# The last gated MLP's gate and value products as seven half-size block products

## The reference, cut to what matters

```python
def swiglu_ffn(h, w_ffn_in, w_ffn_out):
    gate, up = jnp.split(h @ w_ffn_in, 2, axis=-1)
    return (jax.nn.silu(gate) * up) @ w_ffn_out
...
    x = _layer_norm(DEEPNORM_ALPHA * x + (1.0 + g_m) * y, ln1_g[l], ln1_b[l])
    h = _normalize(x) * (1.0 + sc_f) + sh_f
    y = swiglu_ffn(h, w_ffn_in[l], w_ffn_out[l])
    x = _layer_norm(DEEPNORM_ALPHA * x + (1.0 + g_f) * y, ln2_g[l], ln2_b[l])
```

## Time and profile before

| | us |
|---|---|
| median of 3 runs (lowest, highest) | 3415.74 (3415.02, 3417.43) |
| span of the profiled execution | 3414.4 |
| PE busy in it | 3335.1 |
| POOL, DVE, ACT busy in it | 1914.8, 1622.3, 757.2 |
| the last MLP from the end of its opening to the last norm | 3044.3 to 3396.2 |

### The profile page before, as it was taken

One profiled execution on the slowest core, in us unless ns is written; L12 is line 12 of the kernel. 1 busy time (PEld: TensorE's weight loads), 2 busy tenths in 40 slices (PEclk: granted clock), 3 DMA queues, 4 the chain that ended last, 5 costly groups with the idle time before them and its releaser, 6 DMA issues.

```text
span 3414.4 us, 46593 instructions
## 1 busy us (share of the span) xinstructions
PE 3335.1 (98%) x19518; PEld 2647.3 (78%) x19518; DVE 1622.3 (48%) x2658; ACT 757.2 (22%) x1595; POOL 1914.8 (56%) x1555
## 2 busy tenths in 40 slices
PE   8999999999999999999999998999999999999998
PEld 6767788986778888888788787788887776778886
DVE  6544434548444344343532756463346756541123
ACT  2242011347420112000202532110003225120001
POOL 7526666731266666766665003776675645756662
PEclk9999999999999999999999999999999999999999
DMA  5203333230033343332233002333324634422221
GB/s 169 87 25 111 108 127 136 79 103 26 26 111 108 126 136 98 125 123 92 93 96 108 8 3 81 124 99 99 96 90 163 203 99 174 142 75 99 87 99 37
DMA packets 253681, 340.76 MB, mean 100 GB/s; under 512 B 9761, under 2 KB 186145, under 8 KB 250913
## 3 DMA queue, kind: packets, MB, share of 16 engines
q1 hardware_dynamic: 230960, 301.51, 27.2%
q10 hardware_dynamic: 22512, 36.28, 3.1%
HBM read 308.15 MB, written 25.43 MB: 98 GB/s over the span
## 4 chain that ended last, share of the span: by engine, by line
PE 88%; DVE 6%; POOL 2%; ACT 2%; DMA 1%; issue 1%; ACTq 0%; DVEq 0%; SPq 0%; POOLq 0%
PE bank L125 86%; PE bank L128 2%; POOL wlo L148 1%; DVE scr L148 1%; DMA sq<-gates 1%; DVE st L163 0%; POOL whi L155 0%; DVE p L155 0%; POOL raw L148 0%; ACT L143 0%; DVE al L148 0%; DMA raw<-in_w_mlp_in 0%; ACT ah L143 0%; DVE x L148 0%; DVE BK L148 0%
## 5 line engine op out<-in xcount | busy, mean ns | idle before, releaser
L148 POOL TENSOR_TENSOR wlo<-raw,whi 128x512 fp32r<-128x512 f32 x962 | 1297.4, 1379 | 20.1
L155 POOL TENSOR_SCALAR whi<-raw 128x1024 fp32r<-128x1024 f32 x481 | 548.6, 1159 | 1354.7 <-PE bank L125 668.5
L125 PE MATMUL bank<-ah,whi 128*128 128x512 f32 x2408 | 958.8, 398 | 11.3 <-ACT ah L143 4.5
L125 PE MATMUL bank<-ah,wlo 128*128 128x512 f32 x2408 | 951.8, 395 | 0.0
L125 PE MATMUL bank<-al,whi 128*128 128x512 f32 x2408 | 940.4, 395 | 1.0 <-DVE al L158 1.0
L125 PEld LDWEIGHTS bank<-ah,whi 128*128 128x128 f32 x2408 | 451.7, 188 | 132.3 <-ACT ah L143 8.2
L125 PEld LDWEIGHTS bank<-al,whi 128*128 128x128 f32 x2408 | 451.5, 188 | 112.3 <-DVE al L158 1.8
L125 PEld LDWEIGHTS bank<-ah,wlo 128*128 128x128 f32 x2408 | 451.7, 188 | 110.3 <-issue 0.2
L125 PE MATMUL bank<-hh,whi 128*128 128x512 f32 x1040 | 412.5, 397 | 0.0
L125 PE MATMUL bank<-hl,whi 128*128 128x512 f32 x1040 | 410.9, 395 | 0.0
L125 PE MATMUL bank<-hh,wlo 128*128 128x512 f32 x1040 | 410.8, 395 | 0.0
(11 more groups left out here) (456 smaller groups left out, 3978.1 us busy)
## 6 DMA issues: line engine op xcount, KB each, us to landing
raw<-in_w_in SPq DMA_DIRECT2D x34, 1024.0 KB, 5.3
raw<-in_w_mlp_in SPq DMA_DIRECT2D x32, 1024.0 KB, 5.5
raw<-in_w_mlp_out SPq DMA_DIRECT2D x32, 1024.0 KB, 7.3
raw<-in_w_ada SPq DMA_DIRECT2D x24, 1024.0 KB, 5.3
raw<-in_ffn_w_gate SPq DMA_DIRECT2D x22, 1024.0 KB, 5.5
raw<-in_ffn_w_up SPq DMA_DIRECT2D x22, 1024.0 KB, 5.4
raw<-in_ffn_w_down SPq DMA_DIRECT2D x22, 1024.0 KB, 5.0
raw<-in_w_ffn_in SPq DMA_DIRECT2D x22, 1024.0 KB, 5.1
```

Of the source, the lines that this page charges most:

```text
L125: return self.eng.matmul(out, lhsT, rhs, start=start, stop=stop, skip_group_check=True)
L148: return IDLE if self.eng is None else self.eng.tensor_tensor(out, a, b, op)
L155: return self.eng.tensor_scalar(out, a, s1, s2, op0, op1)
```

## The change

Groups 1 to 5 of the last MLP no longer take their gate and value slabs through `lin`. These 18 slabs (four in each of groups 1 to 4, two in group 5) are loaded as before, but as the kind "pairs". A slab of 1024 x 256 weights is seen as 2 x 2 blocks A11, A12 (output tile 0, input rows 0-511 and 512-1023), A21, A22 (output tile 1), and the activations as 2 x 2 blocks of 512 features x 256 tokens. The 2 x 2 block product is done with seven block products (Strassen's form in Winograd's order) instead of eight. Each of the seven is 4 x 3 = 12 matmuls of 128x128 weights on 256 columns, so a slab has 84 of them. Details:

- POOL makes four block sums S1 = A22+A21, S2 = S1-A11, S3 = A11-A21, S4 = A12-S2 (each 128x512; S1, S2, S4 into a tile each, one copy of each for all slabs; S3 in place of A21) and the low parts of A11 and A12. It does S1, the two low parts, S2, S3, S4, in that order.
- ACT makes the seven high parts (each 128x512) in the order A11, A12, S1, S2, A22, S4, S3, and DVE the other five low parts.
- The `whi` and `wlo` buffers are cut into 12 pieces of 128x512; a slab uses seven, and a piece is free when the product that read its predecessor is done.
- PE puts the seven products (0 to 6) into three banks as halves of 256 columns. Product 3 adds onto product 0, 5 onto 2 and 6 onto 3; ACT copies the intermediate states to SBUF (128x256 each: "P1" after product 0, "P5" after product 2, "U2" after 3, "P4" after 4), and PE waits for P1 before product 3, for P5 before product 5 and for U2 before product 6. DVE finishes the two tiles with an addition each (`pair_first_dve` after product 5, `pair_second_dve` after product 6).
- Silu now works on the finished tile in SBUF, and the product of gate and value is SBUF by SBUF into `scr`.
- Once, in group 0, the activations' combinations are made: ACT writes eight value tiles in `ln1_act`, DVE four sums of 128x1024, ACT four high parts, DVE four low parts (products 2, 3, 4 and 6 use them). Those of product 2 overwrite a quarter of `ah` and `al` and so wait for the last matmul of group 0's value slab.

The order in which ACT and DVE interleave this work is written out in `paired_act` and `paired_dve`. The rest of the program issues the same instructions as before. The diff, cut to its core:

```diff
+    BLOCKS = "A11", "A12", "S1", "S2", "A22", "S4", "S3"
+    OPENS, CLOSES = (0, 1, 2, 4), (1, 4, 5, 6)
...
+    def pair_pe(self, e, key, W, c0, after=None, first=False):
+        P, C, D = self.P, self.C, self.D
+        src = W[0:1024, c0:c0 + 256].rearrange("(k p) n -> p k n", p=128)
+        i, _ = self.load("pairs", src, 8, 256, after)
...
+        banks = []
+        for n in range(3):
+            bank, free = self.ps.take(key, n)
+            e.wait_ge(*free)
+            banks.append(bank)
+        a, c, b, m = banks[0][:, 0:256], banks[0][:, 256:512], banks[1][:, 0:256], banks[2][:, 0:256]
+        for n, out in enumerate((b, a, c, b, m, c, b)):
+            e.wait_ge(*self.low_at(s, n))
+            if first and n in (2, 3, 4, 6):
+                e.wait_ge(*D.at(key[0], "tokens", n))
+            if n == 3:
+                e.wait_ge(*C.at(key, "P1"))
+            elif n == 5:
+                e.wait_ge(*C.at(key, "P5"))
+            elif n == 6:
+                e.wait_ge(*C.at(key, "U2"))
+            hi, lo = self.piece(self.whi, q + n), self.piece(self.wlo, q + n)
+            for k in range(4):
+                xh, xl = self.token_block(n, k)
+                e.mm(out, hi[:, k, :], xh, k == 0 and n in self.OPENS, False)
+                e.mm(out, hi[:, k, :], xl, False, False)
+                t = e.mm(out, lo[:, k, :], xh, False, k == 3 and n in self.CLOSES)
+            t.then_inc(*P.up(key, "product", n))
+            self.piece_free[q + n] = P.now()
+    def pair_sums_pool(self, g, s):
+        G, b, used = self.G, lambda name: self.block_of(s, name), lambda name: self.low_at(s - 1, self.BLOCKS.index(name))
+        g.wait_ge(*used("S1"))
+        g.tt(b("S1"), b("A22"), b("A21"), ADD).then_inc(*G.up("sum", s, "S1"))
+        for n in self.BY_POOL:
+            q = self.pair_at.get(s, (0, 0))[1] + n
+            g.wait_ge(*self.C.at("high", s, n))
+            g.tt(self.piece(self.wlo, q), b(self.BLOCKS[n]), self.piece(self.whi, q).bitcast(F), SUB).then_inc(
+                *G.up("low", s, n))
+        g.wait_ge(*G.at("sum", s, "S1"))
+        g.wait_ge(*used("S2"))
+        g.tt(b("S2"), b("S1"), b("A11"), SUB).then_inc(*G.up("sum", s, "S2"))
+        g.tt(b("S3"), b("A11"), b("A21"), SUB).then_inc(*G.up("sum", s, "S3"))
+        g.wait_ge(*used("S4"))
+        g.wait_ge(*G.at("sum", s, "S2"))
+        g.tt(b("S4"), b("A12"), b("S2"), SUB).then_inc(*G.up("sum", s, "S4"))
+    BY_POOL = 0, 1
+    def low_at(self, s, n):
+        return (self.G if n in self.BY_POOL else self.D).at("low", s, n) if s >= 0 else (None, 0)
+    def pair_high_act(self, a, s):
+        i, q = self.pair_at.get(s, (0, 0))
+        for n, name in enumerate(self.BLOCKS):
+            a.wait_ge(*self.free_piece(q + n))
+            a.wait_ge(*(self.raw_in[i % self.NRAW].at(i) if name[0] == "A" else self.G.at("sum", s, name)))
+            a.f(self.piece(self.whi, q + n), self.block_of(s, name), ACT.Copy).then_inc(*self.C.up("high", s, n))
+            yield
+    def pair_low_dve(self, d, s):
+        i, q = self.pair_at.get(s, (0, 0))
+        for n, name in enumerate(self.BLOCKS):
+            if n in self.BY_POOL:
+                continue
+            d.wait_ge(*self.C.at("high", s, n))
+            d.tt(self.piece(self.wlo, q + n), self.block_of(s, name), self.piece(self.whi, q + n).bitcast(F),
+                 SUB).then_inc(*self.D.up("low", s, n))
+            self.raw_free[i] = self.D.now()
+            yield
+    def pair_parts_act(self, a, key, m1, m2, free1, free2):
+        P, C = self.P, self.C
+        X, Y, Z = (self.ps.of(key, n) for n in range(3))
+        a.wait_ge(*P.at(key, "product", 0))
+        a.wait_ge(*free1)
+        a.f(m1[:, 0:256], Y[:, 0:256], ACT.Copy).then_inc(*C.up(key, "P1"))
+        yield
+        a.wait_ge(*P.at(key, "product", 2))
+        a.wait_ge(*free2)
+        a.f(m2[:, 256:512], X[:, 256:512], ACT.Copy).then_inc(*C.up(key, "P5"))
+        yield
+        a.wait_ge(*P.at(key, "product", 3))
+        a.f(m1[:, 256:512], Y[:, 0:256], ACT.Copy).then_inc(*C.up(key, "U2"))
+        yield
+        a.wait_ge(*P.at(key, "product", 4))
+        a.f(m2[:, 0:256], Z[:, 0:256], ACT.Copy).then_inc(*self.ps.give(C, key, 2))
+        C.mark(key, "P4")
+        yield
+    def pair_first_dve(self, d, key, m1):
+        d.wait_ge(*self.C.at(key, "U2"))
+        d.wait_ge(*self.P.at(key, "product", 5))
+        d.tt(m1[:, :], m1[:, :], self.ps.of(key, 0)[:, :], ADD).then_inc(*self.ps.give(self.D, key, 0))
+    def pair_second_dve(self, d, key, m2):
+        d.wait_ge(*self.C.at(key, "P4"))
+        d.wait_ge(*self.P.at(key, "product", 6))
+        m = m2[:, :].rearrange("p (h t) -> p h t", h=2)
+        u = self.ps.of(key, 1)[:, 0:256].unsqueeze(1).to_broadcast([128, 2, 256])
+        d.tt(m, m, u, ADD).then_inc(*self.ps.give(self.D, key, 1))
...
+    def token_sums_dve(self, d, name):
+        D, (v11, v12, v21, v22) = self.D, self.token_values()
+        d.wait_ge(*self.C.at(name, "token value", 7))
+        d.tt(v11, v12, v11, SUB).then_inc(*D.up(name, "sum of tokens", 2))
+        d.wait_ge(*D.now())
+        d.tt(v12, v22, v12, SUB).then_inc(*D.up(name, "sum of tokens", 6))
+        d.wait_ge(*D.now())
+        d.tt(v22, v22, v11, SUB).then_inc(*D.up(name, "sum of tokens", 3))
+        d.wait_ge(*D.now())
+        d.tt(v21, v21, v22, SUB).then_inc(*D.up(name, "sum of tokens", 4))
...
+    def hidden_high_act(self, a, name, T, g, i):
+        if g > 1:
+            a.wait_ge(*self.P.at((name, "down", g - 2), 7))
+        a.wait_ge(*self.D.at(name, "made", g, i))
+        a.f(T["hh"][:, g % 2, i, :], self.scr.of(name, "h", g, i)[:, :], ACT.Copy).then_inc(
+            *self.C.up(name, "hh", g, i))
+    def hidden_low_dve(self, d, name, T, g, i):
+        d.wait_ge(*self.C.at(name, "hh", g, i))
+        d.tt(T["hl"][:, g % 2, i, :], self.scr.of(name, "h", g, i)[:, :], T["hh"][:, g % 2, i, :].bitcast(F),
+             SUB).then_inc(*self.scr.give(self.D, name, "h", g, i))
+    def paired_act(self, a, name, T, g, tiles, more):
+        D, some, s = self.D, self.some, self.pair_first.get(name, 0) + 4 * (g - 1)
+        for p0 in range(0, len(tiles), 2):
+            pair = (p0, p0 + 1)
+            m = [T["gt"][i] for i in pair]
+            parts = self.pair_parts_act(a, (name, "gate", g, p0), *m, *(D.at(name, "made", g - 1, i) for i in pair))
+            s += 1
+            high = self.pair_high_act(a, s)
+            some(parts, 1)
+            if p0:
+                self.hidden_high_act(a, name, T, g, p0 - 2)
+                self.hidden_high_act(a, name, T, g, p0 - 1)
+            some(high, 1)
+            some(parts, 1)
+            some(high, 1)
+            some(parts, 1)
+            some(high, 1)
+            some(parts, 1)
+            run(high)
+            keys = [(name, "h", g, i) for i in pair]
+            parts = self.pair_parts_act(a, (name, "value", g, p0), *(self.scr.of(*k) for k in keys),
+                                        *(self.scr.room(*k) for k in keys))
+            s += 1
+            within = p0 + 2 < len(tiles)
+            high = self.pair_high_act(a, s)
+            some(parts, 1)
+            for i in pair:
+                self.paired_silu_act(a, name, T, g, i)
+            some(high, within)
+            some(parts, 1)
+            some(high, within)
+            some(parts, 1)
+            some(high, within)
+            some(parts, 1)
+            if within or more:
+                some(high, 4 if within else 3)
+        for i in pair:
+            self.hidden_high_act(a, name, T, g, i)
+        if more:
+            run(high)
+    def paired_dve(self, d, name, T, g, tiles, more):
+        C, D, some, s = self.C, self.D, self.some, self.pair_first.get(name, 0) + 4 * (g - 1)
+        def made(p0):
+            for i in (p0, p0 + 1):
+                up = self.scr.of(name, "h", g, i)
+                if i > p0:
+                    self.pair_second_dve(d, (name, "value", g, p0), up)
+                d.wait_ge(*C.at(name, "silu", g, i))
+                d.wait_ge(*D.now())
+                d.tt(up[:, :], T["gt"][i][:, :], up[:, :], MUL).then_inc(*D.up(name, "made", g, i))
+        for p0 in range(0, len(tiles), 2):
+            m1, m2 = T["gt"][p0], T["gt"][p0 + 1]
+            s += 1
+            low = self.pair_low_dve(d, s)
+            if p0:
+                made(p0 - 2)
+                some(low, 1)
+                self.hidden_low_dve(d, name, T, g, p0 - 2)
+                self.hidden_low_dve(d, name, T, g, p0 - 1)
+                some(low, 1)
+            else:
+                some(low, 2)
+            self.pair_first_dve(d, (name, "gate", g, p0), m1)
+            D.mark(name, "gate", g, p0)
+            run(low)
+            s += 1
+            low = self.pair_low_dve(d, s)
+            self.pair_second_dve(d, (name, "gate", g, p0), m2)
+            D.mark(name, "gate", g, p0 + 1)
+            up = [self.scr.take(name, "h", g, i)[0] for i in (p0, p0 + 1)]
```

(68 more changed lines are left out.)

116 lines of the change are left out of this document (91 added, 25 removed).

## The result

The changed kernel takes 3429.43 us (median of 5 runs, 3427.93 to 3429.98); the kernel before, run beside it, 3415.74. The ratio is 1.0042, with a 95% interval of 1.0030 to 1.0053: slower by 13.7 us. The forecast was slower by 19.9 us, 3435.6. The profiled execution spans 3428.1 us, 13.7 more than the one before.

What follows compares the result with a forecast made beforehand. PE bounds the kernel before; after the change, a loop through POOL, ACT and DVE, lengthened by DVE-POOL collisions, stalls it. PE's saving -22.5, handover +5.2, loop +36.2, group 5 +1.0 give +19.9: 3435.6 us, range 3393 to 3450.

Steps and rivals of the forecast that it cites:

- PE's own saving: 18 slabs: 84 short matmuls at 0.118 us, 9.95 us a slab in place of 11.20, saving 22.5 us.
- Prices on DVE, ACT and POOL: Slab work: DVE low parts 0.65 us alone, 1.72 beside POOL; POOL 1.26 alone, 1.68 beside DVE; ACT 0.63 per 128x512.
- reading the blocks in runs of 128 values: POOL's block reads: priced like other reads; a fifth slower would lengthen the loop 1.3 us in 12 slabs, +15.
- the 1.3 that I had named as a sign: DVE's low parts of slabs and hidden tiles: 1.3 us or more in the mean would show the forecast right.
- strict-turns rival: DVE and POOL in strict turns, 1.91 us a pair in place of 1.72, 13.7 more: 3449 us; chance 7%.
- The loop: Groups 1 to 4: A11 rounding to the next takes 13.6 us through POOL, ACT, DVE; stalls 9.05 a group, +36.2.
- The handover: Group 0 to first slab of group 1: PE waits for product 2's low part behind DVE's activation sums, +5.2 us.
- The clock: Whole kernel: full speed expected, as in the opening with 5.5 us of idle PE; nothing taken.
- Group 5: Slabs 1 and 2 only: POOL's split of the down slab ends late, at 20.9 us, +1.0 us.
- The sum: Whole kernel: -22.5 + 5.2 + 36.2 + 1.0 = +19.9 us, 3435.6 us.
- PE stays the bound: Rival: in the groups' slabs a schedule misses collisions, full saving of 22.5 us, 3393 to 3398 us; chance 24%.

Runs made afterwards that it cites:

- e2: The changed kernel with POOL's four block sums cut to 8 of 512 columns in all slabs but the first (values wrong): 3394.33 us.
- e8: e5 with three low parts (A11, A12, S1) on POOL and four on DVE: 3418.58 us.
- e1: The changed kernel with DVE's five low parts of a slab reading an idle PSUM bank in place of the high part (values wrong): 3395.63 us.
- e5: The changed kernel with ACT's copies P1, P5, U2 put ahead of roundings and Silu that wait, plus e4's changed order ending group 0: 3401.64 us.
- e4: The changed kernel with group 0's end reordered: product 2's activations rounded after three slab roundings, DVE's second-pair work ahead of four low parts: 3426.11 us.
- e10: e5 with DVE's two low parts of hidden tiles moved behind the fourth slab's low parts: 3406.47 us.
- e6: The changed kernel, orders as they are, with all seven low parts on DVE and only the four sums on POOL: 3424.20 us.

## Why the prediction was right, step by step

- **PE's own saving**: -22.5 forecast. e2 shows slabs at 9.80 in place of 9.95: 18 x 1.40 = -25.2. The distance of 0.118 came from rows 4, where the trace shows neither a wait nor a slower clock; why it is a little larger there stays open.
- **Prices on DVE, ACT and POOL** held: hidden low parts on DVE 1.45 in the mean, the sums on POOL 1.49 to 1.74, ACT's roundings 0.62 to 0.63. Block sums with DVE idle beside them take 1.27 to 1.31 us in e8, as the low parts do, so reading the blocks in runs of 128 values costs POOL nothing extra. e1 shows the collisions as the cause. The low parts of a slab came to 1.25 in the mean of all, 1.05 for those of A22 and S3, under the 1.3 that I had named as a sign; the hidden ones to 1.50. The strict-turns rival (1.91 a pair) fell: in the timeline two in a row take 3.48 us, 1.74 each, close to the 1.72 of rows 6.
- **The loop**: 13.6 us forecast, 13.4 measured, through the same instructions. Stalls in the order in which I named them: forecast 1.3, 2.2, 1.95, 3.5 (8.95; my 9.05 has 0.1 of rounding); measured from PE's starts 1.0, 2.0, 1.8, 2.3, and 0.4 in shorter gaps, that is 7.5 in place of 9.05 a group, 30.1 in place of 36.2. The largest was mis-sized: DVE's addition for tile 3 ended 42.8 us into the group (3185.4), not at 44.9. POOL's last sum was 0.9 us ahead of my schedule, and DVE's three low parts behind it took 4.0 us in place of 5.1: POOL was not subtracting beside the first two, as I had assumed, but still rounding the down slab (3179.64 to 3182.57), and they took 0.92 and 1.52 us.
- **The handover**: 5.2 forecast, all of it a wait for product 2's low part. Group 1 takes 7.2 us more than group 2: 4.2 of stall and some 4 of slow clock, less the 1.0 of the first wait in slab 3, which it doesn't have.
- **The clock**: I took nothing, since a stretch with 5.5 us of idle PE in the opening had kept 1.00. Wrong step. 6.9 us at 1.2 GHz around the end of the handover's stall put 27 matmuls 0.096 us further apart, 2.6 us; one episode of 3.4 us at the end of group 1 cost 1.5; two in group 3 cost 3.0, of which the wait behind the first gave 1.5 back (0.2 in place of 1.8), so that group 3 takes 1.6 us more than groups 2 and 4. Together some 5.7 us.
- **Group 5**: +1.0 forecast for the late split; 19.73 in place of 19.6, +0.1.
- **The sum**: -25.2 + 7.2 + 30.1 + 1.6 + 0.1 = +13.8, against +19.9. The places of the stalls were right and their sizes too large; the clock was left out. These errors have opposite signs, and that is luck: by these terms the change without its slow clock would have cost some 8 us (an estimate, 13.8 less 5.7).
- **The rivals**: that PE stays the bound is what e1 and e2 make of it, at 3395.6 and 3394.3, where I had put it at 3393 to 3398. It needs the collisions gone, or POOL's sums with them; e5 shows that order alone takes the kernel to 3401.6.

Left open: why stalls of nearly the same place and length bring a slow clock in group 3 and none in groups 2 and 4 (in e4 and e10 it was group 4). No kernel here isolates it.

## What to carry to other kernels

Fewer matmuls pay only as far as the other engines' chain per slab is shorter than PE's new time; write that chain out once round, with the durations that the instructions have beside each other and not alone. A small copy that PE waits for must not stand in its engine's queue behind anything that waits for a third engine: reordering ACT's queue alone was worth 24 us here. When moving work between two engines that collide, test the splits on both sides of the one you have, and again when an order has changed: none on GpSimd was a little better than two before ACT's queue was reordered, and 15 us worse after.

## What the runs showed of the hardware that I had not expected

The granted clock fell to half during a wait of PE of 4.0 us behind full work, and in places after two waits of about 2 us; in e5, whose longest wait of PE in the groups is 2.4 us, it never fell before the last norm. The length of a wait alone doesn't tell: in e6 it stayed at 1.00 in groups 2 to 4 through waits of 3.3 us, and in e10 it fell in group 4 after one of 2.3 us and not in groups 2 and 3 after the same. In the opening, with 5.5 us of idle in sum before the change but in pieces of at most 1.1 us, it stayed at full speed before and after the change.
